# An opening on two DMA queues, the last expert's gated values in halves, quarter-wise rms scaling and a new split of the final stores in a one-core transformer kernel

## The reference

```python
u = jnp.einsum("bsd,de->bse", x, w_in)            # first product of the program
hb = jax.nn.silu(xb @ w1[e]) * (xb @ w3[e])       # one expert, then hb @ w2[e]
y = xf * lax.rsqrt(jnp.mean(xf * xf, axis=-1, keepdims=True) + RMS_EPS)
return (y * g.astype(jnp.float32) + ...)          # rms_norm: y * g
```

## Time and profile before

| | |
|---|---|
| median of 3 runs | 1743.29 us (1742.96 to 1743.67) |
| the profiled execution: its time, its span | 1743.21 us, 1741.9 us |
| PE busy | 1699.2 us, 98% of the span |
| DVE, ACT, POOL busy | 793.8, 623.6, 126.0 us |
| HBM read | 542.19 MB, 312 GB/s over the span |

### The profile page before, as it was taken

One profiled execution on the slowest core, in us unless ns is written; L12 is line 12 of the kernel. 1 busy time (PEld: TensorE's weight loads), 2 busy tenths in 40 slices (PEclk: granted clock), 3 DMA queues, 4 the chain that ended last, 5 costly groups with the idle time before them and its releaser, 6 DMA issues.

```text
span 1741.9 us, 23928 instructions
## 1 busy us (share of the span) xinstructions
PE 1699.2 (98%) x9970; PEld 1111.2 (64%) x9970; DVE 793.8 (46%) x1528; ACT 623.6 (36%) x1197; POOL 126.0 (7%) x150
## 2 busy tenths in 40 slices
PE   9999999998999999999999989999999999999998
PEld 9974334433234984344343333887999899789997
DVE  6961111111003791111111012866888677868885
ACT  6541100000003660100010002656666564756665
POOL 0000000000001000000000001231111011301101
PEclk9999999999899999999999999999999999999999
DMA  9869999999999799999999999534555544435550
GB/s 384 340 255 413 424 428 427 428 427 427 426 424 420 291 378 394 422 430 428 428 428 427 426 426 419 198 125 142 186 178 194 194 169 146 145 134 176 187 194 24
DMA packets 56948, 544.90 MB, mean 313 GB/s; under 512 B 6400, under 2 KB 6400, under 8 KB 8832
## 3 DMA queue, kind: packets, MB, share of 16 engines
q1 hardware_dynamic: 56416, 542.14, 77.2%
q10 hardware_dynamic: 416, 1.13, 0.2%
HBM read 542.19 MB, written 1.05 MB: 312 GB/s over the span
## 4 chain that ended last, share of the span: by engine, by line
PE 77%; DMA 17%; DVE 4%; issue 1%; ACT 1%; POOL 0%; ACTq 0%; SPq 0%; DVEq 0%
PE PS L1324 24%; DMA ring<-in_w 17%; PE PS L444 13%; PE PS L446 13%; PE PS L445 13%; PE PS L1306 2%; PE PS L1378 2%; PE PS L1524 2%; PE PS L1038 1%; PE PS L1340 1%; PE PS L2068 1%; PE PS L1392 1%; DVE wl L415 1%; PE PS L1497 1%; DVE sm L658 0%
## 5 line engine op out<-in xcount | busy, mean ns | idle before, releaser
L1324 PE MATMUL PS<-ring,F 128*64 128x512 f32 x1984 | 446.7, 598 | 23.7 <-DMA ring<-in_w 15.6
L415 DVE TENSOR_TENSOR wl<-ring,wh 128x512 fp32r<-128x512 f32 x496 | 359.4, 743 | 136.5 <-ACT wh L409 133.7
L409 ACT ACTIVATE wh<-ring 128x512 fp32r<-128x512 f32 x504 | 314.9, 630 | 266.5 <-PE PS L446 245.7
L1324 PEld LDWEIGHTS PS<-ring,F 128*64 128x64 f32 x1984 | 140.3, 137 | 306.8 <-issue 273.9
L444 PE MATMUL PS<-xh,wl 128*128 128x256 f32 x1120 | 322.3, 288 | 0.7 <-DVE wl L415 0.7
L445 PE MATMUL PS<-xl,wh 128*128 128x256 f32 x1120 | 316.8, 283 | 0.0
L446 PE MATMUL PS<-xh,wh 128*128 128x256 f32 x1120 | 316.8, 283 | 0.0
L444 PEld LDWEIGHTS PS<-xh,wl 128*128 128x128 f32 x1120 | 214.7, 192 | 3.7 <-DVE wl L415 2.0
L445 PEld LDWEIGHTS PS<-xl,wh 128*128 128x128 f32 x1120 | 214.8, 192 | 0.5
L446 PEld LDWEIGHTS PS<-xh,wh 128*128 128x128 f32 x1120 | 214.7, 192 | 0.0
L444 PE MATMUL PS<-wh,xl 128*128 128x512 f32 x320 | 129.7, 405 | 0.2 <-DVE F L2609 0.2
(11 more groups left out here) (453 smaller groups left out, 2048.2 us busy)
## 6 DMA issues: line engine op xcount, KB each, us to landing
ring<-in_w SPq DMA_DIRECT2D x98, 2048.0 KB, 25.3
ring<-in_w SPq DMA_DIRECT2D x68, 1024.0 KB, 11.1
ring<-in_ffn_up SPq DMA_DIRECT2D x44, 1024.0 KB, 4.9
early<-in_w SPq DMA_DIRECT2D x16, 2048.0 KB, 26.2
F<-in_w SPq DMA_DIRECT2D x15, 2048.0 KB, 26.1
F<-in_w SPq DMA_DIRECT2D x22, 1024.0 KB, 10.5
ring<-in_ffn_down SPq DMA_DIRECT2D x22, 1024.0 KB, 4.9
ZX<-in_w SPq DMA_DIRECT2D x7, 2048.0 KB, 26.3
```

The source lines that it names most:

```text
L409: act.e.activation(self.wh[:, p % NPIECE, :], self.piece_source(p), ACT.Copy).then_inc(*self.up("w_hi", p))
L415: dve.e.tensor_tensor(self.wl[:, p % NPIECE, :], self.piece_source(p), f32(self.wh[:, p % NPIECE, :]), ALU.subtract).then_inc(*self.up("w_ ...
L1324: t = pe.e.matmul(PS[64 * half:64 * half + 64, bank, :], lhs(k), weights[:, a:a + 512], start=(k == 0), stop=(k == 7))
```

## The change

1. **Opening.** SP issues x and then pieces 2 and 3 of the first chunk; ACT issues pieces 0 and 1 itself, ahead of everything else. DVE fills 128 columns of F with ones, and PE runs 9 products of those instead of 7 of the identity. DVE, not ACT, makes `wh` of piece 0, ahead of its `xl` work. ACT's order becomes xh 0, xh 1, wh 1, xh 2, xh 3, wh 2, wh 3; DVE's becomes wh 0, xl 0, xl 1, wl 0, xl 2, xl 3, wl 1 to 3. The filling products are one of 128 columns after q = 1 and none after q = 3.
2. **Last expert of each layer.** `hh` is made in two halves of 256 columns, each transposed to its own bank (4 and 6) and copied to `hT` on its own; the w2 product waits for the first half at its blocks 0 and 1, and for the second at 2 and 3. The statistics of bank (0,0) move ahead of DVE's copy of the second result half.
3. **Rms scaling.** DVE's 512 columns become two instructions of 256, each with its own signal to the transposes.
4. **End.** For h = 1 ACT scales columns 0 to 383 and issues their store itself; DVE scales 384 to 1023, which SP stores as one transfer of 320 KB. ACT's is 192 KB.

```diff
@@ opening
-        for j, pieces in enumerate((slice(0, 512), slice(512, 1024), slice(1024, 2048))):
-            self.sp.e.dma_start(self.chunk(0)[:, pieces], self.source(0)[:, pieces]).then_inc(self.first_in[j][0], 16)
+        self.sp.e.dma_start(self.chunk(0)[:, 1024:2048], self.source(0)[:, 1024:2048]).then_inc(self.first_in[2][0], 16)
+    def scalar_first_pieces(self):
+        for j in range(2):
+            pieces = slice(512 * j, 512 * j + 512)
+            self.act.e.dma_start(self.chunk(0)[:, pieces], self.source(0)[:, pieces]).then_inc(self.first_in[j][0], 16)
...
+        pe.wait_ge(at("ev_awake"))
+        for _ in range(9):
+            pe.e.matmul(PS[:, 7, 0:128], self.F[:, 0:128], self.F[:, 0:128], start=True, stop=True)
         pe.wait_ge(at("consts", "ident"))
-        for _ in range(7):
-            pe.e.matmul(PS[:, 7, 0:128], self.ident[:, :], self.ident[:, :], start=True, stop=True)
...
-            if q % 2:
-                self.tensor_busy(7, 1)
+            if q == 1:
+                pe.e.matmul(PS[:, 7, 0:128], self.ident[:, :], self.ident[:, :], start=True, stop=True)
...
-        for q in range(4):
+        self.scalar_first_pieces()
+        for q in range(2):
             high(q)
-        for n in range(4):
+        self.scalar_split(1)
+        for q in range(2, 4):
+            high(q)
+        for n in range(2, 4):
             self.scalar_split(n)
...
-        for q in range(4):
+        dve.e.memset(self.F[:, 0:128], 1.0).then_inc(*up("ev_awake"))
+        dve.wait_ge(self.first_in[0])
+        dve.e.tensor_copy(self.wh[:, 0, :], self.piece_source(0)).then_inc(*up("w_hi_first"))
+        for q in range(2):
             low(q)
-        for n in range(4):
+        self.vector_split(0)
+        for q in range(2, 4):
+            low(q)
+        for n in range(1, 4):
             self.vector_split(n)
@@ last expert
+    def tensor_turn_last(self, layer):
+        pe, hh = self.pe, self.moe_views()["hh"]
+        for part in range(2):
+            pe.wait_ge(self.at("hidden", layer, 15, part))
+            for j in range(2):
+                a = 256 * part + 128 * j
+                t = pe.e.transpose(self.last_turned(part)[:, j * 128:j * 128 + 128], hh[:, a:a + 128], self.ident[:, :])
+            t.then_inc(*self.up("hid_turned", layer, 15, part))
...
+                if c == 0 and kk % 2 == 0:
+                    pe.wait_ge(self.at("hid_t", layer, 15, kk // 2))
...
             if ex == 15:
-                dve.wait_ge(at("combined_single", layer))
+                self.vector_stats(f"moe{layer}", 0, 0)
+                dve.wait_ge(self.expert_done(layer, ex, 2), at("combined_single", layer))
                 e.tensor_copy(self.last_result(1), PS[:, 4, :]).then_inc(*up("y_last", layer, 1))
@@ rms scaling
-        self.dve.e.tensor_scalar(self.Z[:, 1, 0:512], self.X[:, 1, 0:512], self.sm[:, 501:502], None, ALU.mult).then_inc(
-            *self.up("scaled_first", stage))
+        for q in range(2):
+            c = slice(256 * q, 256 * q + 256)
+            self.dve.e.tensor_scalar(self.Z[:, 1, c], self.X[:, 1, c], self.sm[:, 501:502], None, ALU.mult).then_inc(
+                *self.up("scaled_first", stage, q))
@@ end
+        columns = slice(0, 384 if h else 512)
...
+        if h:
+            act.wait_ge(at("y_ready0", 1))
+            act.e.dma_start(self.out[128:256, columns], self.Z[:, 1, columns]).then_inc(self.s_out, 16)
...
-        for h in range(2):
-            for d in range(2):
...
+        for d in range(2):
+            c = slice(d * 512, d * 512 + 512)
+            self.sp.wait_ge(self.at(f"y_ready{d}", 0))
+            self.sp.e.dma_start(self.out[0:128, c], self.Z[:, 0, c]).then_inc(self.s_out, 16)
+        self.sp.wait_ge(self.at("y_ready1", 1))
+        self.sp.e.dma_start(self.out[128:256, 384:1024], self.Z[:, 1, 384:1024]).then_inc(self.s_out, 16)
```

More of the change, by code:

```diff
@@ L1393, in tensor_turn_hidden, with last_turned @@
         t.then_inc(*self.up("hid_turned", layer, ex))
+    def last_turned(self, part):
+        return self.PS[:, 6 if part else 4, 256 * part:256 * part + 256]
+    def tensor_turn_last(self, layer):
[6 more added lines that the diff above has]
+            t.then_inc(*self.up("hid_turned", layer, 15, part))
     def tensor_turn_gates(self, layer, q):
@@ L1647, in moe_scalar @@
                 self.scalar_gathered(layer, q + 1)
-            act.wait_ge(at("hid_turned", layer, ex))
-            act.e.activation(v["hT"], PS[:, 4, :], ACT.Copy).then_inc(*up("hid_t", layer, ex))
+            if ex < 15:
+                act.wait_ge(at("hid_turned", layer, ex))
+                act.e.activation(v["hT"], PS[:, 4, :], ACT.Copy).then_inc(*up("hid_t", layer, ex))
+            else:
+                for part in range(2):
+                    act.wait_ge(at("hid_turned", layer, 15, part))
+                    act.e.activation(v["hT"][:, 256 * part:256 * part + 256], self.last_turned(part), ACT.Copy).then_inc(
+                        *up("hid_t", layer, 15, part))
             if o == 0:
@@ L1830, in moe_vector @@
             dve.wait_ge(self.expert_done(layer, ex, 1), at("silu", layer, ex))
-            e.scalar_tensor_tensor(out=v["hh"], in0=self.silu(ex), scalar=0.5, in1=PS[:, 5, :], op0=ALU.mult,
-                                   op1=ALU.mult).then_inc(*up("hidden", layer, ex))
+            for part in ((slice(0, 512),) if ex < 15 else (slice(0, 256), slice(256, 512))):
+                e.scalar_tensor_tensor(out=v["hh"][:, part], in0=self.silu(ex)[:, part], scalar=0.5, in1=PS[:, 5, part],
+                                       op0=ALU.mult, op1=ALU.mult).then_inc(
+                    *up("hidden", layer, ex, *((part.start // 256,) if ex == 15 else ())))
             if o == 0 and q < 7:
@@ L1853, in vector_after_experts @@
     def vector_after_experts(self, stage):
-        for h in range(2):
-            self.vector_stats(stage, h, 0)
+        self.vector_stats(stage, 1, 0)
         for h in range(2):
@@ L3155, in vector_finish @@
         for h in range(2):
-            dve.wait_ge(at("rstd", ("down1", h)), at("y_gain_last") if h else at("y_gain", 0, 1))
-            dve.e.tensor_scalar(self.Z[:, h, 512:1024], self.Z[:, h, 512:1024], self.sm[:, 500 + h:501 + h], None,
+            columns = slice(384 if h else 512, 1024)
+            dve.wait_ge(at("rstd", ("down1", h)), *((at("y_gain", 1, 0), at("y_gain_last")) if h else (at("y_gain", 0, 1),)))
+            dve.e.tensor_scalar(self.Z[:, h, columns], self.Z[:, h, columns], self.sm[:, 500 + h:501 + h], None,
                                 ALU.mult).then_inc(*up("y_ready1", h))
@@ L3172, in scalar_finish @@
         act, at, up = self.act, self.at, self.up
+        columns = slice(0, 384 if h else 512)
         act.wait_ge(at("rstd", ("down1", h)), at("y_gain", h, 0))
-        act.e.activation(self.Z[:, h, 0:512], self.Z[:, h, 0:512], ACT.Copy,
+        act.e.activation(self.Z[:, h, columns], self.Z[:, h, columns], ACT.Copy,
                          scale=self.sm[:, 500 + h:501 + h]).then_inc(*up("y_ready0", h))
+        if h:
+            act.wait_ge(at("y_ready0", 1))
+            act.e.dma_start(self.out[128:256, columns], self.Z[:, 1, columns]).then_inc(self.s_out, 16)
     def sync_store(self):
-        for h in range(2):
-            for d in range(2):
-                c = slice(d * 512, d * 512 + 512)
-                self.sp.wait_ge(self.at(f"y_ready{d}", h))
-                self.sp.e.dma_start(self.out[h * 128:h * 128 + 128, c], self.Z[:, h, c]).then_inc(self.s_out, 16)
+        for d in range(2):
[4 more added lines that the diff above has]
+        self.sp.e.dma_start(self.out[128:256, 384:1024], self.Z[:, 1, 384:1024]).then_inc(self.s_out, 16)
         self.sp.e.wait_ge(self.s_out, 64)
```

23 lines of the change are left out of this document (15 added, 8 removed).

## The result

The changed kernel takes 1746.47 us (median of 17 runs, 1744.14 to 1747.82) beside 1743.15 for the kernel before: a ratio of 1.0018, interval 1.0012 to 1.0024, or 3.3 us more. The forecast was 1741.8 us with a range from 1740.3 to 1743.6.

What follows compares the result with a forecast made beforehand. The chain of waits ran 77% through TensorE, 17% through DMA and 4% through VectorE. Terms 1.06 + 0.1 + 0.33 + 0 = 1.5 us, of which 1.4 kept, took 1743.21 to 1741.8 us, range 1740.3 to 1743.6.

Steps and rivals of the forecast that it cites:

- I take x at 6.8 and the product at 7.9: a gain of 0.5: Opening: x's second half in at 6.8 us, first product at 7.9 instead of 8.40; gain between 0.17 and 1.0.
- the bound of 7.13: Opening: x in at 7.13 us if both issuers share evenly, 512 KB more at 410 GB/s taking 1.28 us.
- 0.2 MB or 0.5 us: Opening: shortfall from full DMA rate in the first five busy slices, taken as room a second queue can fill.
- the smallest gain, 0.17 us: Opening: gain if x waits for all 1536 KB; the rule on issuing engines spoke for this end.
- The stall of 0.56: Opening: PE's wait for `cols` before 20.56 us, to vanish as ACT issues `cols` near 8.5 instead of 9.72.
- the opening's 1.06 us of gain: Opening in total: 0.5 us from an earlier first product plus 0.56 from the `cols` stall; ends 0.0 and 1.56.
- rival C: Slower: PE at half clock through the opening, 5.1 us for a 10.2 us stretch, giving 1746.9 us; chance 0.05.
- The weight stream: Behind the opening: compute starts the stream, so whatever the opening saves moves the stream and all behind it equally.
- Last expert: Both layers, 0.1 us: w2 product starts 0.6 to 0.9 us earlier but waits for its third chunk.
- Rms scaling: Three places, 0.33 us in all: transposes start 0.13 us earlier, 0.11 gained on PE each; ends 0 and 0.4.
- End: Final stores: gain 0, as the queue is already full near 400 GB/s; possibly 0.4 us gained or 0.1 lost.

Runs made afterwards that it cites:

- sp_mixed: Changed kernel, all four weight pieces issued by SP in the order piece 0, x's first half, piece 1, x's second half, pieces 2 and 3: 1744.24 us, ratio 1.0007.
- x_two_queues: Changed kernel with all four weight pieces issued by SP and x's second half issued by ACT: 1742.86 us, ratio 0.9997.
- rest_only: Changed kernel with the opening of before, so last expert, rms scaling and end alone: 1743.02 us, ratio 0.9998.
- after_again: Changed kernel unaltered, run again for a second profile: 1746.81 us, ratio 1.0018.
- open_only: Kernel before with the edits of the opening alone: 1746.36 us, ratio 1.0020.
- act_pieces: Kernel before with only the issue of weight pieces 0 and 1 moved from SP to ACT: 1745.75 us, ratio 1.0018.
- open_sp: Changed kernel with all four pieces of the first weight chunk issued by SP behind x: 1742.90 us, ratio 0.9998.
- after_fill: Changed kernel with 16 opening fillers for 9 and 4 for 1 after the first transposes: 1744.81 us, ratio 1.0008; again 1744.93 us, 1.0010.
- after_third: Changed kernel unaltered, run once more on the same chip as the third set: 1746.29 us, ratio 1.0021.
- sp_gap: Changed kernel with all four weight pieces issued by SP and 3 opening fillers in place of 9: 1742.84 us, ratio 0.9998.

## Why the prediction was wrong

**The step that failed** is the opening's "I take x at 6.8 and the product at 7.9: a gain of 0.5". x's second half was ready for its transposes at 8.77 us, 2 us later than taken and 1.6 beyond the bound of 7.13; the product came at 9.62, a loss of 1.22. x's transfers took 2.5 us more to land on the median (6.7 in place of 4.2), where 0.9 later was forecast. The bound was built on 410 GB/s for the 512 KB that come in between. But weights do not start at that rate. The earlier trace rows showed it, a fall to 82 GB/s, and I read it as a pause "when x is in and the weights have not begun". It is the way that the weights' first transfers run, with packets of 178 ns where x's took 86, and the fall goes where they go: 5.75 to 6.75 us before, 3.0 to 5.5 in the changed kernel, 2.5 to 4.5 in `sp_mixed`, 5.5 to 7.25 in `x_two_queues`. Why they start slowly, no run here shows. The "0.2 MB or 0.5 us" of room was no room.

By the Trainium skill, page DMA: Bandwidth & Descriptors, section Issuing engines are not separate DMA queues, transfers of both issuers interleave on the same 16 engines. The runs agree. I hung the smallest gain, 0.17 us, on it; what came was a loss, since what interleaves is slow.

**`cols`.** The stall of 0.56 is gone, but not for the reason given: `cols` was issued at 10.00 and not 8.5, later than before, and DVE got it at 19.82. TensorE came 1.2 us later and found it there. So the opening's 1.06 us of gain is a loss of 0.59 in the profile.

**The clock, rival C**, had a chance of 0.05 and a price of 5.1 us for a full stretch. By the profiles it is part of what happened. The record of the granted clock begins where the half pace of the start ends: in the 11 of the 14 profiles in which TensorE is at work at that moment, the spacing of its instructions goes from 0.21 to 0.11 or 0.12 us there (at 4.86 us in the kernel before, 7.00 in `rest_only`, which has the same opening). In seven profiles TensorE waited over 1.3 us for x behind its fillers. In three of those the record begins at 9.61 to 10.68 us, in two the clock fell back to 0.50 (from 8.43 us in `after_again`, from 7.70 in `open_only`), two showed neither. In the seven with a shorter wait or none it begins by 7.20, without a fall in the opening. That filling the waits gives 1.6 of the 3.3 us is shown by runs.

That the clock is what the fillers change in the timed runs is argued, not shown. By the lag at the first expert product the profiles with fillers (0.75 and 1.63 us) are no better than those without (0.57, 1.97 and 1.44). The mean granted clock of the timed runs is higher with fillers (median 0.999 against 0.996), but the profiles put that difference elsewhere: a stretch of 7 to 10 us at 0.50 near 437 us, which the kernel before has too, is missing in both with fillers. Layer 0's experts, in which it lies, take 410.0 and 412.0 us in those two, and 410.4 to 411.4 in the three of the changed kernel, so nothing shows its absence as a gain. Sorted afterwards, the 15 of the changed kernel's 39 runs with a mean clock up to 0.995 have a median of 1747.16 us, the other 24 one of 1746.08; that leans to the clock, and 99 runs of the kernel before show no such order. The remaining 1.7 us go with late x, as in `act_pieces`, and in part with fillers that outlast x's arrival.

The Trainium skill, page TensorE: Matmul & The Clock Gate, Part 1, says that the same kernel can show a different number of slow products from run to run. The trace agrees: behind the fillers one profile of the changed kernel has none, one has them from 8.7 us, one from 7.1.

**The weight stream.** The forecast said that what the opening saves or loses moves all behind it. 0.57 of 0.59 us arrived at 143 us, and in each of the 12 other profiles the lag at 28 us arrives there within 0.06. That part was right. Behind it single profiles can't be compared to 1 us: from that product to POOL's last root they take 1593.7 to 1596.3 us. Over layer 0's experts 0.47 more were lost in this profile, but that stage varies by itself: it took 410.9 us in the kernel before, 411.4 in this profile, 410.4 in `after_again`, 412.0 in `open_sp` and 410.0 in `after_fill`.

**Last expert** 0.1: right in mechanism, with 0.01 measured in layer 0. The 0.61 us won in front of the product are lost again before its third chunk comes, 0.38 of them as PE's wait right in front of it.

**Rms scaling** 0.33, measured 0.12 and 0.15 at the first two places, and the third lost 0.15 before the first product behind it, where DVE's `wl` waits for ACT's `wh` (9.37 us from the residual to `wl`, before 9.22). The first two are differences of the lag over some 150 to 190 us. The step was right for the transposes, and wrong in taking PE's side of it for the chain's at all three.

**End** 0: right, within 0.1.

**Still open** is the gap between `sp_mixed` and the changed kernel. Both are late by the same at 28 us in their profiles (29.47, and 29.45 in `after_third`), yet the timed runs stand 2.0 us apart. So a cost of the second queue that no profile shows is not ruled out: `x_two_queues` excludes it for x alone, and no run has weights on a second queue without x late. No profile of the changed kernel is over 2.0 us late at 143 us, where the runs cost 3.3. Its three profiled executions (1744.14, 1744.56, 1744.42 us) are also some 2 us below its median, while those of the kernels with fillers are not. Something in the unprofiled runs of the two-queue opening is worse than any trace here shows; a longer or later half clock would fit, and nothing shows it.

## What to carry to other kernels

What the first product needs is to be alone on the DMA engines: put it first, and let nothing whose start is slow in among it. From a second queue that cost 2.6 and 3.3 us here; from the same queue it made the data as late, and 1.0 us that the runs do not tell from nothing. A dip in the DMA rate that comes with the start of a stream is no room: it moves with the stream. Where a wait in front of the first products can't be avoided, cover it with fillers: here seven more of them, and three behind the first transposes, gave back 1.6 of 3.3 us. Without a late x a wait cost nothing (`sp_gap`), so first mend what is late.

## What the runs showed of the hardware

- Two queues with x on both moved 336 to 418 GB/s from 3.0 to 5.25 us; x on one and weights on the other 180 to 319 with the engines as busy.
- Packets of 2 KB took 86 ns for x and 178 ns for the first weights behind it (kernel before); 99 and 164 ns side by side (changed kernel); the weights' took 87 ns from 5.75 us on there.
- The record of the granted clock begins from 4.28 us (`open_only`) to 10.68 us (`sp_mixed`), where the spacing of TensorE's instructions goes from 0.21 to 0.11 or 0.12 us. Before it the view prints 1.00, while eight transposes take 1.94 us (`sp_gap`, 4.86 us): read the spacing of rows there.
- Half pace in the first transposes without any wait before them (`rest_only`: 1.93 us for eight, 1.10 in the profile of before).
- The profiled executions of the changed kernel were 1.9 to 2.3 us below the medians of its three sets; for a change of 0.2% the runs decide, and the trace only says where to look.
